# One core, two transformer blocks in fp32: a new order of work at the entry into RWKV and in memory attention

## What is computed

```python
h = x
proj = rms_norm(h, norm_mix_w) @ w_in                  # RWKV part and differential-attention part
y_rwkv = rwkv7_group(p_rwkv, ...)                      # 8 heads of 64, decay and in-context rate from low-rank products
y_diff = diff_attn_group(p_diff, ...)                  # 4 heads of 128, softmax(q1k1) - lam*softmax(q2k2), then rms_norm
h = h + concat([y_rwkv, y_diff]) @ w_out
h = h + memory_cross_attn(rms_norm(h), rms_norm(mem))  # 4 heads of 256 over 256 memory tokens, q, k, v, o products of 1024x1024
h = h + relu(rms_norm(h) @ w_up)**2 @ w_down           # then two more layers with GLA, sliding-window attention and MLPs
```

## Time and profile before

| | us |
|---|---|
| median of 3 runs | 2114.72 (2114.07 to 2118.31) |
| the profiled execution's own time | 2125.83 |
| its span, first to last instruction | 2123.7 |
| PE busy | 2037.3 (96%) |
| DVE busy | 997.6 (47%) |
| ACT busy | 732.3 (34%) |
| POOL busy | 133.8 (6%) |
| PE's share of the chain that ended last | 91% |
| mean granted TensorE clock | 0.976 of full |

### The profile page before, as it was taken

One profiled execution on the slowest core, in us unless ns is written; L12 is line 12 of the kernel. 1 busy time (PEld: TensorE's weight loads), 2 busy tenths in 40 slices (PEclk: granted clock), 3 DMA queues, 4 the chain that ended last, 5 costly groups with the idle time before them and its releaser, 6 DMA issues.

```text
span 2123.7 us, 28770 instructions
## 1 busy us (share of the span) xinstructions
PE 2037.3 (96%) x12656; PEld 1654.1 (78%) x12656; DVE 997.6 (47%) x1249; ACT 732.3 (34%) x1056; POOL 133.8 (6%) x139
## 2 busy tenths in 40 slices
PE   6999898889799999999999999999999999999997
PEld 5877677678688888887888888888887678888886
DVE  5476457546444323435645543234345755423433
ACT  4233534324343213334323343124233644312321
POOL 3054000000000000001000000000001210000000
PEclk9999799999999999999999999999998999999999
DMA  7312211123623323322231222232232212332221
GB/s 228 100 60 82 78 52 50 44 100 95 76 89 99 99 81 98 100 81 81 80 100 40 80 89 95 94 99 92 87 100 69 71 56 84 99 99 92 88 80 40
DMA packets 163355, 181.84 MB, mean 86 GB/s; under 512 B 4661, under 2 KB 154181, under 8 KB 162848
## 3 DMA queue, kind: packets, MB, share of 16 engines
q1 hardware_dynamic: 159552, 166.74, 24.5%
q0 software_dynamic: 3680, 13.28, 2.9%
HBM read 172.66 MB, written 7.34 MB: 85 GB/s over the span
## 4 chain that ended last, share of the span: by engine, by line
PE 91%; DVE 5%; ACT 2%; issue 1%; DMA 1%; SPq 0%; DVEq 0%; ACTq 0%
PE M L1242 25%; PE M L1243 24%; PE M L1244 24%; PE X L518 2%; PE M L1303 1%; PE M L1305 1%; PE M L1304 1%; PE M L518 1%; PE M L1559 1%; PE X L1547 1%; DVE w_lo L1854 1%; DMA h<-in_x_dram 1%; PE X L1536 1%; PE M L1379 1%; PE X L1441 0%
## 5 line engine op out<-in xcount | busy, mean ns | idle before, releaser
L1854 DVE TENSOR_TENSOR w_lo<-raw,w_hi 128x2048 fp32r<-128x2048 f32 x155 | 354.1, 2285 | 352.5 <-ACT w_hi L1616 352.5
L1616 ACT ACTIVATE w_hi<-raw 128x2048 fp32r<-128x2048 f32 x155 | 293.9, 1896 | 414.9 <-PE M L1244 361.7
L1242 PE MATMUL M<-f,w_hi 128*128 128x512 f32 x768 | 304.2, 396 | 0.0
L1244 PE MATMUL M<-u,w_hi 128*128 128x512 f32 x768 | 303.0, 395 | 0.0
L1243 PE MATMUL M<-u,w_lo 128*128 128x512 f32 x768 | 303.0, 395 | 0.0
L1243 PE MATMUL M<-f,w_lo 128*128 128x512 f32 x768 | 303.0, 395 | 0.0
L1242 PE MATMUL M<-u,w_hi 128*128 128x512 f32 x768 | 303.0, 395 | 0.0
L1244 PE MATMUL M<-f,w_hi 128*128 128x512 f32 x768 | 303.0, 395 | 0.0
L1243 PEld LDWEIGHTS M<-f,w_lo 128*128 128x128 f32 x768 | 144.7, 188 | 34.4 <-issue 0.7
L1242 PEld LDWEIGHTS M<-f,w_hi 128*128 128x128 f32 x768 | 144.7, 188 | 34.3 <-issue 0.7
L1661 ACT ACTIVATE nt<-ut 128x512 f32<-128x512 f32 x96 | 60.7, 632 | 320.5 <-DVE ut L1927 320.5
(11 more groups left out here) (483 smaller groups left out, 3278.0 us busy)
## 6 DMA issues: line engine op xcount, KB each, us to landing
raw<-in_w_up_dram SPq DMA_DIRECT2D x48, 1024.0 KB, 5.4
raw<-in_w_down_dram SPq DMA_DIRECT2D x48, 1024.0 KB, 5.1
raw<-in_w_in_dram SPq DMA_DIRECT2D x13, 1024.0 KB, 5.4
raw<-in_a_w_in_dram SPq DMA_DIRECT2D x12, 1024.0 KB, 5.4
raw<-in_w_mk_dram SPq DMA_DIRECT2D x4, 1024.0 KB, 5.2
raw<-in_w_mv_dram SPq DMA_DIRECT2D x4, 1024.0 KB, 5.2
raw<-in_w_out_dram SPq DMA_DIRECT2D x4, 1024.0 KB, 5.1
raw<-in_w_mq_dram SPq DMA_DIRECT2D x4, 1024.0 KB, 5.7
```

Source lines behind the costliest of these rows:

```text
L1242: mm(dst, wh, xh, start=start, stop=False)
L1244: return mm(dst, wh, xl, start=False, stop=stop)
L1616: nc.scalar.activation(w_hi[:, n % 2, :, 0:cols], raw[:, n % 4, :, 0:cols], ACT.Copy).then_inc(S["w_hi_ready"], 1)
L1854: TTO(w_lo[:, n % 2, :, 0:cols], raw[:, n % 4, :, 0:cols], w_hi[:, n % 2, :, 0:cols].bitcast(f32), ALU.subtract).then_inc(S["w_lo_ready"], 1)
```

## The change

- **Entry.** Unit 14 of the differential attention takes four key pieces (0 to 3) in place of two, unit 15 takes 4, 5, 6 and then 7, and piece 8 comes after the last product with v. Pieces 9 and 10 come between and behind the low-rank products.
- **Low-rank products.** Their order is zw, za of pair 0, zw, za of pair 1, a piece, zw, za of pair 2, zw, za of pair 3. Each waits only for what it needs: the banks of the attention, and tanh alone, not for the sigmoid of the gate's input. ACT takes tanh and sigmoid straight after unit 15.
- **Last head's norm.** Its square (`sq3`), its product with ones, logarithm, exponential and multiply (`dn`) become steps of the RWKV order.
- **Weights.** `hi` and `lo` of MK+2 move ahead of RWKV; later ones come earlier in its order (FILL_AT).
- **x** is loaded by SP instead of POOL, after the last value piece, four tiles ahead of the WOB blocks and four behind. WOB's ring is turned so that its first two chunks lie in banks 0 and 1.
- **Memory attention.** Heads come between the chunks of MQ, their scores always in X banks 0 and 1, the products with the values in M banks 2 and 3; MQ uses a ring of two banks, 0 and 1. MO becomes two wide halves: MOA (contraction over heads 0 and 1, ring 0 and 1) can start before heads 2 and 3 are done, MOB follows. Each has 8 chunks of 12 matmuls; `h` is therefore updated twice, 8 more DVE additions.

```diff
+WOB_RING = (2, 3, 0, 1)
-... ("WOB", 2, 4, ANY), ("MQ", 4, 2, ANY), ("MO", 4, 2, ANY), ...
+... ("WOB", 2, 4, WOB_RING), ("MQ", 4, 2, (0, 1)), ("MOA", 2, 4, (0, 1)), ("MOB", 2, 4, ANY), ...
-RW_ORDER = [f"{e}.{st}".split(".") + [hp] for st in ("zw", "za") for e in "pa" for hp in range(4)]
+RW_ORDER = [[e, st, hp] for e in "pa" for hp in range(4) for st in ("zw", "za")]
+RW_ORDER.insert(4, ["p", "fill", 9])
+RW_ORDER += [["p", "fill", 10], ["p", "dn", 0]]
+RW_ORDER.insert(RW_ORDER.index(["a", "za", 0]) + 1, ["a", "sq3", 0])
-FILL_AT = {7: -1, 8: 1.5}
-FILL_AT.update({9 + i: 5 + 4.5 * i for i in range(11)})
+FILL_AT = {11: 3}
+FILL_AT.update({12 + i: 8 + 5 * i for i in range(8)})
...
-for _f in range(1, 10):
-    _p = -6 if _f == 1 else FILL_AT[4 * _f if _f < 8 else 32 + 8 * (_f - 8)]
+_merged += [(-1, 4, ["d", "ev"]), (1.5, 0, ["a", "dn"]), (6.5, 0, ["d", "dn"])]
+for _f in range(2, 10):
+    _p = 0.6 if _f == 2 else FILL_AT[4 * _f if _f < 8 else 32 + 8 * (_f - 8)]
...
+            entry = {("zw", 0): ("da_exp", 32), ("zw", 1): ("da_at", 16), ("za", 1): ("da_o", 4),
+                     ("zw", 2): ("da_ln", 3), ("za", 2): ("da_ln", 3), ("kk2", 0): ("rw_p", 14), ("gate", 0): ("rw_lora", 2)}
...
+            sp.wait_ge(S["acc_done"], DONE[N_WOA])
+            for c in range(KT):
+                if c == 4:
+                    load_wide(N_WOB, mix_w, 0)
+                sp.dma_start(h[:, c, :], A["x"][:, c, :]).then_inc(S[f"ld_x{c}"], 16)
...
-                    rw_fill(2 * (u - 14))
-                    rw_fill(2 * (u - 14) + 1)
+                    for j in (range(0, 4), range(4, 7))[u - 14]:
+                        rw_fill(j)
...
-            rw_fill(5)
-            diff_norm(3)
-            rw_fill(6)
-            wait("da_y", 4)
-            wait("rw_p", 14)
-            wait("rw_lora", 2)
+            rw_fill(8)
...
+            chunk(N_MQ + 1, 0, x2_hi, x2_lo)
+            mem_scores(0)
+            chunk(N_MQ + 1, 1, x2_hi, x2_lo)
+            chunk(N_MQ + 2, 0, x2_hi, x2_lo)
+            mem_scores(1)
+            wait("ld_rel", 48)
+            mm(X[3][0:16, 0:384], relx[:], onehot[:], start=True, stop=True).then_inc(S["bias_mm"], 1)
+            chunk(N_MQ + 2, 1, x2_hi, x2_lo)
+            mem_transposes(0)
+            chunk(N_MQ + 3, 0, x2_hi, x2_lo)
+            mem_attend(0)
+            mem_scores(2)
+            chunk(N_MQ + 3, 1, x2_hi, x2_lo)
+            mem_transposes(1)
+            mem_scores(3)
+            mem_attend(1)
+            mem_transposes(2)
+            wait("ma_lo", 2)
+            for part in range(2):
+                if part:
+                    wait("ma_lo", 4)
+                mem_out(0, part, 2)
+                mem_out(1, part, 2)
+            mem_attend(2)
+            mem_transposes(3)
+            mem_out(2)
+            mem_attend(3)
+            for c in range(3, KT):
+                mem_out(c)
+            wait("ma_lo", KT)
+            for c in range(KT):
+                chunk_part(N_MOB + c // 4, c % 4, o_hi, o_lo, 0, 1, at=4, flat=True)
...
             act.wait_ge(S["rw_p"], 14)
             nc.scalar.activation(p_rw[:, 13, :], p_rw[:, 13, :], ACT.Sigmoid).then_inc(S["rw_lora"], 1)
...
```

More of the change, by code:

```diff
@@ L187, in rw_place @@
         sets = ((0, 1), (2, 3), (4, 5), (1, 2)) if st in RW_QUAD else tuple((b,) for b in range(6))
+        if hp == 3 and st in ("Y", "gate", "var"):
+            sets = [bs for bs in sets if max(bs) < 4]
         best = min(sets, key=lambda bs: (max(free[b] for b in bs), -sum(free[b] for b in bs)))
@@ L194, in rw_place @@
             free[b] = at[(e, *op)]
-    return banks, after
-RW_BANKS, RW_BANKS_AFTER = rw_place()
+    return banks, after, user
+RW_BANKS, RW_BANKS_AFTER, RW_BANKS_LAST = rw_place()
 def program(nc, A, out):
@@ L487, in rwkv_pe @@
                 fs = slice(hp * P, hp * P + P)
+                if (st, hp) in entry:
+                    wait(*entry[(st, hp)])
                 if st == "zw":
                     wait("ld_lora", 48)
+                    wait("rw_lora", 1)
                     last = mm(bank[:], lora[0:64, fs], p_rw[0:64, 12, :], start=True, stop=True)
@@ L492, in rwkv_pe @@
                     last = mm(bank[:], lora[64:128, fs], p_rw[64:128, 12, :], start=True, stop=True)
+                elif st == "dn":
+                    wait("da_sq", 4)
+                    last = mm(bank[:], C("ones"), de_sq[:], start=True, stop=True)
                 elif st == "gate":
@@ L1479, in mem_scores, with mem_transposes @@
                 last.then_inc(S["ma_score"], 1)
-            mem_scores(0)
-            mem_scores(1)
-            wait("ld_rel", 48)
-            mm(X[3][0:16, 0:384], relx[:], onehot[:], start=True, stop=True).then_inc(S["bias_mm"], 1)
-            for hd in range(4):
+            def mem_transposes(hd):
                 wait("ma_p", hd + 1)
@@ new lines, in _ @@
+            dve.wait_ge(S["kv_hi"], 2)
+            TTO(mv_lo[:], vf[:], mv_hi[:].bitcast(f32), ALU.subtract).then_inc(S["kv_lo"], 1)
+            mem_maxima(0)
+            mem_query(3)
+            mem_probabilities(0)
+            query_part(3)
+            lo(N_MQ + 3)
+            mem_query(4)
+            query_part(4)
+            mem_maxima(1)
+            mem_query(5)
+            mem_probabilities(1)
+            query_part(5)
+            lo(N_MOA)
+            mem_pt_lo(0)
+            mem_query(6)
@@ new lines, in _ @@
+            query_part(6)
+            mem_o_lo(0)
+            mem_maxima(2)
+            mem_query(7)
+            mem_probabilities(2)
+            query_part(7)
+            lo(N_MOA + 1)
+            mem_pt_lo(1)
+            mem_maxima(3)
+            mem_o_lo(1)
+            mem_probabilities(3)
+            mem_pt_lo(2)
+            resid_chunk(N_MOA, 0, 0)
+            resid_chunk(N_MOA, 0, 1)
+            mem_o_lo(2)
+            mem_pt_lo(3)
+            resid_chunk(N_MOA, 0, 2)
+            mem_o_lo(3)
@@ new lines, in _ @@
+            resid_chunk(N_MOA, 0, 3)
+            lo(N_MOB)
+            for c in range(4, KT):
+                resid_chunk(N_MOA, 0, c)
+            for b in range(2):
+                lo(N_MOB + b + 1)
+                for c in range(4 * b, 4 * b + 4):
+                    resid_chunk(N_MOB, 0, c)
+                    if c:
+                        norm_step(2, c - 1, 2, h[:, c - 1, :], V("norm_mlp_w", c - 1), mem_of[0][1], mem_of[0][0])
+            norm_step(2, 7, 2, h[:, 7, :], V("norm_mlp_w", 7), mem_of[0][1], mem_of[0][0])
```

209 lines of the change are left out of this document (118 added, 91 removed).

## The result

| | before | after |
|---|---|---|
| median | 2114.39 us (4 runs, 2111.90 to 2118.31) | 2085.00 us (4 runs, 2083.09 to 2088.53) |
| ratio | | 0.9861, 95% interval 0.9839 to 0.9883 |
| the profiled execution's own time | 2125.83 us | 2083.24 us |
| its span, its mean granted clock | 2123.7 us, 0.976 | 2081.2 us, 0.991 |

The change makes the kernel 1.4% faster, by 29.4 us; forecast were 29.5 and a median of 2085.2. So this close hit is in part luck: what the change is worth lies at 24 to 29 us.

The account below looks back on a forecast made before the run. PE was taken to bound the kernel, so gains come only where it waits or runs slowly. Entry 18 plus memory 13 is 31, less 1 to 2 kept back: 29.5, so 2114.7 becomes 2085.2 us; 8-in-10 range 2078 to 2099.

Parts of the forecast that it names:

- Rival A: Whole kernel: the forecast itself holds, 29.5 us gained, median 2085.2 us; chance 0.60.
- B: Memory attention: DVE becomes the bound, PE waits on query evacuations, stretch gains only 5 or 6 us; 2093 us, chance 0.16.
- C: Entry: three gaps of about 2 us in the first pair's chain, each followed by half clock; gain 12, 2091 us, chance 0.12.
- D: Entry: low-rank products don't go side by side in the new order, costing 2.6 us; 2088 us, chance 0.05.
- E: RWKV: regular pauses sink its clock, at 0.70 the kernel gets slower than before, 2122 us; chance 0.03.
- F: Later stages: the gains are taken back by a stage behind a transfer, result within 0.2%; chance 0.04.
- Entry: Attention's end into RWKV: first pair's RKT mask 17.3 us earlier; 18 us gain taken, between 12 and 24.
- The pairs: Low-rank products at the entry: four pairs side by side, 1.06 us a pair, between 0.85 and 1.7.
- One piece less, up to 1.4 us: RWKV after the first pair's mask: one key piece already done that PE no longer owes, up to 1.4 us.
- Memory: Memory attention through output product: 14.4 us by the timeline, 13 us gain taken, between 6 and 16.
- x and WOB's ring: x loaded by SP and WOB's turned banks: 0 us taken, bounds 0 and 4.7; 2.8 us wait for `h` stays.
- The profiled execution: Whole kernel under profiling: 2125.8 less 29.5 gives 2096.3 us, its 11 us distance to the median carried over.

Follow-up runs that it names:

- e10: Changed kernel plus three DVE moves (low part of MK+2, WOA chunk 4's evacuation, query chunk 7's low part, each earlier); 2084.0 us, 0.9850 of before.
- e3: Changed kernel with the low-rank products in the old order, none beside another; 2089.4 us, 0.9869 of before.
- e2: Changed kernel with the memory attention and undivided output product of before, so the entry part alone; 2102.2 us, 0.9935 of before.
- e4: Changed kernel with x loaded by GpSimd as before and WOB's first block loaded early again; 2083.6 us, one run.
- e1: Kernel before with only the memory attention and divided output product of the change; 2100.6 us, 0.9925 of before.
- e11: Changed kernel with two key pieces in units 14 and 15 as before, pieces 5 to 8 behind unit 15; 2090.9 us, 0.9871 of before.
- e12: Changed kernel with two pieces a unit, old low-rank order and last head's norm ahead of tanh, all together; 2088.1 us, 0.9892 of before.
- e14: Kernel before with both parts of MK+2 made ahead of RWKV and pieces 7 and 8 ahead of the low-rank products; 2107.5 us, 0.9962 of before.
- e15: Kernel before with the joint wait taken apart, low-rank products waiting for tanh only; 2113.1 us, 0.9986 of before.
- e5: Changed kernel with the last head's norm ahead of tanh and sigmoid as before; 2088.4 us, 0.9861 of before.

## Why the prediction held, step by step

**Sum.** Forecast 29.5 us (18 + 13, less 1.5 kept back); at MLP1's norm product the two executions of the changed kernel are 30.2 and 27.2 us ahead of before, the medians 29.4 and 24.1. That the first median lies 0.2 us from the forecast is luck: the entry was taken 1.7 us too high, memory 0.8 too low, 1.5 were kept back for no wait in particular, and the errors cancel. The 4 us (0.2%) that I took for what a measurement can tell were too few: two series of one kernel lie 5.7 us apart. Rival A was the case; no wait for a query evacuation (B), one short fall of the clock in the first pair's chain, behind the wait of 1.9 us, not three (C: 0.96 over 224 to 264), the products side by side (D, in the timeline), RWKV's clock at 0.95 as before (E), nothing taken back later (F: from MLP1's norm product to that ahead of the sliding-window stage before takes 955.2 us, after 953.9).

**Entry: 18 forecast, 16.3 and 13.4 measured at MQ.** By kind, the 16.3 are 10.7 us less lost at half clock, 3.8 less idle and 1.8 of other work saved; the 13.4 are 6.1, 5.1 and 2.2. My ceiling of 26 had some 10 lost at half clock, 13 idle and 3 side by side: the clock's share was right for the first execution. Of the idle time ahead of the mask, 12.9 us, 7.1 went, but between the mask and MQ it grew from 25.4 to 28.6, so 3.8 are the net. The chain up to the mask is right but for one term. Transposes of unit 14 at 205.5 (forecast 205.2), no gap in unit 15 (0.3), product with v till 215.0 (214.8). Then piece 8 starts at 216.2 where I had it end: DVE's evacuation of pieces 4 and 5 stands ahead of the low part of MK+2 and waits 1.60 us for the store of the staging buffer. I had counted that evacuation at its own length alone, without the wait for the buffer that it fills. All that follows is 1.5 us late and otherwise as forecast: scan 221.9 (220.4), ACT's block of MK+3 till 230.0 (228.5), PE's waits of 1.23 and 1.91 (1.1 and 2), mask 251.8 (250.2); with the first norm product 0.1 later, 15.9 against 17.3. e10 moves the evacuation behind the low part and gets 0.9 to 1.3 of it back.

**The pairs** were mis-sized: 1.06 us a pair taken; measured are two passes of 0.43 (218.35, 218.78, 219.21) and 3.83 us for all four with their starts, against 4.24. The price at the lower bound was right. Also, in the kernel before the last two zw products already ran beside the first two za products (in PE's timeline passes of L490 and L492 alternate from 226.61 to 230.19). Its 9.7 us, most of them at half clock, are twelve passes' time one after the other, some 5.2 us at full clock, so the new order by itself saves about 1.3 against before, where it saves 3.5 against e3. The Trainium skill (TensorEngine Tiling (Array Packing), Key Properties) says that a change of tiling mode drains the engine; here the first product of 64 rows starts 0.21 us behind the last of 128, against 0.12 between two of these.

**One piece less, up to 1.4 us:** not seen. From mask to MQ before takes 224.9, after 224.5 and 227.9, e2 225.0, e4 224.9. What PE no longer owes there is less than what half clock gives and takes, 7.4 us before and 4.2 to 9.3 with the new entry. The two further waits of 2 us for low parts did not come either.

**Memory: 14.4 worked, 13 taken, 13.8 measured.** The timeline put one wait at `mq_lo` of 1.9 us; it is there, 1.85 us at 532.58, and the only one. Half clock behind it costs about what was forecast (532 to 580 at 0.96, 1.9 us). e1 and e2 show the part to be independent of the entry.

**x and WOB's ring: 0.** For x right by e4, for the ring not shown; the wait for `h` stays at 2.7 us.

**The profiled execution: 2096.3 forecast, 2083.2 measured.** The step that failed is an unspoken one: I treated the 11 us between before's profiled execution and its median as a property of profiling. They are 11 us of one stage at clock 0.93 in that execution. Subtracting from the median was right only because it carried this distance over unchanged; the forecast of the profiled time inherited the disturbance.

**The reason for the half clock at the entry** was taken too simply. In the earlier trace rows it follows a gap of 2.1 us in unit 15, and I priced the entry as if closing the gaps closed it. e11, e12, e14 and e15 have the same gap of 2.1 us and full clock behind it; e5 has full clock behind 3.5 us, e14 half clock behind 1.2. What all executions of the new entry share is that little is lost in 198 to 300: 1.7 to 4.9 us against 12.4. In unit 15 PE's list does not decide it alone, since before and e1 have half clock there and e14 and e15 full clock with the same list. What decides it stays open, and so does how much of the 10.7 us that the entry regained at half clock is due to the new order.

## What to carry to other kernels

Ask of every operation on the path ahead of a chain's first step whether it must be there: the two parts of a weight block (4.3 us) that stood between the low-rank products and the scan, and the two pieces that could fill a wait of 4.1 us, were worth more (8.3 us) than the three reorderings that catch the eye (4.3 together). Parts undone one at a time add up only where they lie on one path, so undo them together once. Compare executions by marks inside the program, stage by stage, and count the time lost at half clock: it moved identical code by 3 us here, and 11 us in one stage.

## What the runs showed of the hardware that I had not expected

- The length of one gap does not tell whether the clock falls: 3.47 us of waiting and full clock behind it (e5), 1.23 us and a clock of 0.66 over the next 4 us (e14), 2.1 us in unit 15 with half clock behind it before and in e1 and full clock in e11, e12, e14 and e15. The Trainium skill (TensorE: Matmul & The Clock Gate, HAM oscillation) describes a kernel that waits for data between its groups of products, with waits longer than most of these, and starts at the lower clock behind every one; the traces here agree for some gaps and not for others.
- The same program falls to half clock at different places: in 300 to 490 us it lost 4.2 us in one execution and 9.3 in another, and two of fourteen profiled executions, of two different kernels, ran one stage of 165 us in 176.
- Two products of 64 rows in the two halves of the array cost together what one costs alone, 0.86 us for 512 columns, with starts 0.01 us apart.
- Each of the entry's three table loads has the next operation directly behind it, in ACT's timeline of the changed kernel:

```profile
213.30 1.28 ACT L1783 ACT_TABLE_LOAD   x1
...
214.60 0.63 ACT L1783 ACTIVATE p_rw<-p_rw 64x512 f32<-64x512 f32 x1
215.25 1.28 ACT L1785 ACT_TABLE_LOAD   x1
...
216.54 0.63 ACT L1785 ACTIVATE p_rw<-p_rw 128x512 f32<-128x512 f32 x1
...
224.97 1.28 ACT L626 ACT_TABLE_LOAD   x1
226.26 0.72 ACT L589 ACTIVATE nt<-p_rw,vec 128x512 f32<-128x512 f32 x1
```

  The drain of 1.4 us that the Trainium skill (ScalarE: Activation LUTs, What ACT_TABLE_LOAD costs) adds to each is not there, and counting the load alone was right.
